# A two-layer hybrid attention trunk on one core: GpSimd casts the high part of every weight half by a copy, with its loops written out

## The reference, cut to what matters

```python
for l in range(DEPTH):
    mod = c_act @ w_mod[l] + b_mod[l]
    shift, scale, gate = jnp.split(mod, 3, axis=-1)
    h = x * (1.0 + scale[:, None, :]) + shift[:, None, :]
    p = h @ w_in[l]
    ...
    y = jnp.concatenate([y_nsa, y_gdn, y_sb], axis=-1) @ w_out[l]
    x = _layernorm(DEEPNORM_ALPHA * x + (1.0 + gate[:, None, :]) * y, ln_g[l], ln_b[l])
```

## Time and profile before

| | |
|---|---|
| time, median of 3 | 2987.98 us (2983.08 to 2988.05) |
| the profiled execution, its own time | 2985.01 us |
| its span, first to last instruction | 2983.2 us |
| mean granted TensorE clock | 0.949 |
| PE busy | 2580.8 us, 87% |
| DVE busy | 1493.6 us, 50% |
| ACT busy | 646.7 us, 22% |
| POOL busy | 1491.2 us, 50% |

### The profile page before, as it was taken

The page is one execution under the profiler, slowest core; times in us unless marked ns, Lnnn a source line. Parts: engine busy times, 40 slices in busy tenths (PEclk is TensorE's granted clock), DMA queues, the critical chain, the costliest instruction groups (busy, mean ns, idle before and its releaser), DMA issues.

```text
span 2983.2 us, 40726 instructions
## 1 busy us (share of the span) xinstructions
PE 2580.8 (87%) x14320; PEld 2030.7 (68%) x14320; DVE 1493.6 (50%) x1915; ACT 646.7 (22%) x1168; POOL 1491.2 (50%) x692
## 2 busy tenths in 40 slices
PE   0498879878999999898987999999899999997994
PEld 0376667656777777675875777777677777774773
DVE  8614751575555553565334144144655554457445
ACT  0201210112222223333003022012222222335000
POOL 7155335433444444554762644554444444553774
PEclk9999989998999999998998999999999999998997
DMA  9533343343211112444223311321111112334531
GB/s 357 211 113 107 127 143 127 113 149 99 64 56 56 56 57 76 148 137 170 93 73 115 119 57 58 120 66 55 50 57 57 57 57 63 122 121 161 188 95 71
DMA packets 82892, 314.73 MB, mean 106 GB/s; under 512 B 9974, under 2 KB 10230, under 8 KB 76950
## 3 DMA queue, kind: packets, MB, share of 16 engines
q1 hardware_dynamic: 76608, 295.51, 30.0%
q10 hardware_dynamic: 6108, 16.83, 1.6%
HBM read 303.92 MB, written 8.39 MB: 105 GB/s over the span
## 4 chain that ended last, share of the span: by engine, by line
PE 52%; DVE 20%; POOLq 12%; issue 9%; ACT 3%; DMA 2%; DVEq 1%; ACTq 1%; SPq 0%
DVE arena L1241 12%; PE bank L450 11%; PE bank L452 10%; PE bank L451 10%; POOLq L1198 7%; POOLq L1196 5%; DVE acc L1241 5%; PE bank L831 2%; PE bank L833 2%; PE bank L832 2%; PE bank L430 2%; ACT arena L843 2%; DMA ring<-in_stream 2%; DVE tiny L1241 2%; PE bank L534 1%
## 5 line engine op out<-in xcount | busy, mean ns | idle before, releaser
L1195 POOL TENSOR_TENSOR w_hi<-ring,cst 128x1024 fp32r<-128x1024 f32 (+1 forms) x328 | 622.3, 1897 | 1403.9 <-PE bank L452 892.7
L450 PE MATMUL bank<-h_hi,w_hi 128*128 128x512 f32 x2048 | 894.3, 437 | 47.5 <-POOLq L1198 44.1
L1197 POOL TENSOR_TENSOR w_lo<-ring,w_hi 128x1024 fp32r<-128x1024 f32 (+1 forms) x328 | 802.8, 2448 | 48.0 <-issue 0.4
L452 PE MATMUL bank<-h_hi,w_lo 128*128 128x512 f32 x2048 | 822.4, 402 | 0.9 <-issue 0.9
L451 PE MATMUL bank<-h_lo,w_hi 128*128 128x512 f32 x2048 | 822.5, 402 | 0.0
L450 PEld LDWEIGHTS bank<-h_hi,w_hi 128*128 128x128 f32 x2048 | 400.7, 196 | 156.6 <-POOLq L1198 46.9
L452 PEld LDWEIGHTS bank<-h_hi,w_lo 128*128 128x128 f32 x2048 | 397.8, 194 | 91.5
L451 PEld LDWEIGHTS bank<-h_lo,w_hi 128*128 128x128 f32 x2048 | 400.5, 196 | 82.3 <-issue 13.5
L843 ACT ACTIVATE arena<-bank 128x512 f32<-128x512 f32 (+6 forms) x352 | 165.8, 471 | 1031.9 <-PE bank L452 402.6
L1241 DVE SCALAR_TENSOR_TENSOR acc<-ring,cact,acc 128x1024 f32<-128x1024 f32 x128 | 213.6, 1669 | 45.8 <-DMA ring<-in_stream 29.9
L831 PE MATMUL bank<-w_hi,h_hi 128*128 128x512 f32 x512 | 202.7, 396 | 7.5 <-POOLq L1198 7.5
(11 more groups left out here) (192 smaller groups left out, 2816.9 us busy)
## 6 DMA issues: line engine op xcount, KB each, us to landing
ring<-in_stream SPq DMA_DIRECT2D x480, 512.0 KB, 3.5
yT<-in_mod SPq DMA_DIRECT2D x32, 1024.0 KB, 5.2
arena<-in_x SPq DMA_DIRECT2D x1, 4096.0 KB, 14.2
arena<-in_x ACTq DMA_DIRECT2D x4, 1024.0 KB, 10.0
x_norm<-arena ACTq DMA_DIRECT2D x4, 1024.0 KB, 9.0
arena<-x_norm ACTq DMA_DIRECT2D x4, 1024.0 KB, 9.3
out<-arena SPq DMA_DIRECT2D x4, 1024.0 KB, 3.9
raw<-in_lns ACTq DMA_DIRECT2D x8, 256.0 KB, 5.9
```

The costliest lines, as they stand in the source:

```text
L450: mm(PJ[b][:, :], hi, h_hi[:, k, :], start=(k == 0), stop=False)
L452: last = mm(PJ[b][:, :], lo, h_hi[:, k, :], start=False, stop=(k == KT - 1))
L1195: pool.tensor_tensor(w_hi[:, par, 0:w], ring[:, slot, 0:w], one.broadcast_to((P, w)), ALU.mult)
L1197: pool.tensor_tensor(w_lo[:, par, 0:w], ring[:, slot, 0:w], w_hi[:, par, 0:w].bitcast(F32), ALU.subtract)
```

## The change

The product with ones becomes a copy whose output type is float32r, and four loops of POOL become Python loops, so that all numbers in its waits are constants:

```diff
-            one = ones[:, 0:1]
...
-                pool.tensor_tensor(w_hi[:, par, 0:w], ring[:, slot, 0:w], one.broadcast_to((P, w)), ALU.mult)
+                pool.tensor_copy(w_hi[:, par, 0:w], ring[:, slot, 0:w])
...
-                with pool.Fori(0, KVH) as g:
+                for g in range(KVH):
...
-                with pool.Fori(0, GDN_H) as h:
+                for h in range(GDN_H):
...
-                with pool.Fori(0, SB_H - 2) as h:
+                for h in range(SB_H - 2):
...
-                with pool.Fori(0, TT) as n:
+                for n in range(TT):
```

## The result

The changed kernel takes 2896.27 us (median of 4 runs, 2894.21 to 2901.1), the kernel before 2985.53 us in the same comparison: the ratio is 0.9706, 95% interval 0.9686 to 0.9727, a gain of 2.9% or about 88 us. The prediction was 2947 us with a range of 2924 to 2976: right in direction, and too small by more than half. The profiled execution took 2894.2 us, its span is 2892.4 us, its mean granted clock 0.959 (0.949 before).

A forecast was written before the change was run, and what follows sets the result against it. The kernel was taken as PE-bound with holes (PE busy 87% of the span). Direct waits 13.9, DVE held by POOL 21 and clock 3 sum to 38 us, so 2985.0 - 38 = 2947 us, range 2924 to 2976.

The forecast's parts named there:

- two kinds of holes: PE's waits POOL can touch: 51.6 us for a split itself, and many for DVE (56.0 us at line 621).
- Part D: POOL's written-out loops: branches and register instructions hidden behind POOL's waits, given nothing; late code fetch bound 0 to 3 us.
- the ladder: Delta-rule heads: DVE and POOL instructions hold each other in turn; a shorter product moves the whole chain 0.74 us earlier.
- Part A: PE's 20 direct waits for POOL at lines 450 and 831: shorter splits save 13.9 us.
- Part B: PE's waits for DVE held by POOL, at lines 430, 621, 608 and 778: 21 us saved.
- Part C: PE's lower granted clock behind long waits: mostly stays, 3 us saved, bounds 0 and 8.
- The price of the copy: POOL's copy on 1024 columns: 1.15 us from the int32 CAST row, a saving of 0.74 us per split.
- my lower end: Copy priced as the 512-column MEMSET doubled: 1.04 us, a saving of 0.85 per split.
- shorter ones among the 43 waits: PE's shorter waits for DVE at line 621: about 8 us, counted only in the low end.
- my low end: Forecast's fastest time, 2924 us: a saving of 61 us with cheaper copy, full Part B and 8 of clock.
- rivals 2 and 3: Copy no cheaper, 2985 to 2988 us, chance 0.07; copy in a slow loop, slower at 3067 us, chance 0.07.
- Rival 1: Only direct waits gain, as Part B's hits cancel: 2971 us, chance 0.08.

The follow-up runs named there:

- two pieces: The change, with each half split in two pieces (copy and difference of 512 columns each), PE told after each: 2832.07 us, ratio 0.9512.
- the copy made again: The change, with 605 of the 1024 columns copied a second time before the difference: 2935.46 us, ratio 0.9856.
- the difference with an early signal: The change, copy whole, difference in two instructions of 512 columns, PE told after each: 2854.65 us, ratio 0.9591.
- the copy with a MEMSET behind it: The change, with a MEMSET of 740 columns of the low part between copy and difference: 2918.31 us, ratio 0.9802.
- The product in halves: The kernel before, its loops and product with ones kept, the product made in two instructions of 512 columns: 2968.29 us against 2979.12, ratio 0.9964.
- four-piece run: The change, with each half split in four pieces of 256 columns, PE told after each: 2896.59 us, ratio 0.9715.

## Why the prediction was wrong, point by point

Right were the way the gain takes (PE's holes, not POOL's load), the two kinds of holes, the worthlessness of the loops (Part D), and the order of the ladder. (Part D put the registers and branches at a few tenths of a us per half if nothing covered them. Where POOL went straight on to the next half it stood idle 0.33 to 0.34 us before and 0.31 after, so they cost hundredths.) The forecast fell short in the sizes of all three parts:

| term | predicted | measured |
|---|---|---|
| saving per split | 0.74 us | 0.86 (1935 to 1078 ns mean) |
| Part A, waits for POOL | 13.9 | 25.6 (51.6 to 26.0) |
| Part B, line 430 | 12 | 20.1 |
| Part B, lines 621 and 608 | 6 | 11.9 (65.6 to 53.7) |
| Part B, line 778 | 3.0 | 3.0 |
| Part B, other waits for DVE | 0 | 5.1 |
| Part C, the clock | 3 | 23.6 |

- **The price of the copy.** I had taken the CAST from int32 as the nearest row. Unheld, the float32 copy takes 1.04 us, as long as the MEMSET doubled, my lower end. That alone makes 38 into 44.
- **Part A.** The shift was about right for the first waits of layer 0 (4.03 to 3.10, 3.88 to 3.26), but three things were missing. In stick-breaking, the difference itself had been held by DVE (3.14 us where 2.34 is its own time); an earlier split misses that hold, and the long waits there fell by up to 2 us each. The four waits of 1.2 to 2.0 us vanished entirely, so that eight of my twelve are left. And three waits in the output projection fell from 2.25 to 0.64 us: the copy was issued 3.0 us behind the start of DVE's additions where the product had been issued 2.2 behind it, so it also met less of the first addition (it took 1.45 us, 0.4 over its own time, where the product took 3.16, 1.3 over).
- **Part B.** The discounts were wrong. The full shift, 20 x 0.74 = 14.8, was discounted to 12 because ACT and PE feed these chains. Measured, nine long waits lost 0.88 to 0.95 us, the ten short ones 0.82 to 0.84, and one of 2.90 us went whole. Nothing of the shift was lost. And the "shorter ones among the 43 waits", put at the low end only, belonged in the sum.
- **Part C is the step that failed worst:** 3 us, with a bound of 8, where PE's busy time fell by 23.6. I argued that the long waits of Part A stay long, so the loss behind them stays, and I looked at the waits for POOL alone. In the timeline of PE after the first 125 us, 53 waits of 2 us or more stand before the change and 29 after it. Ten of those that went are the 2.8 us waits at line 430. Behind seven of these the granted clock is now 1.00, each some 1.4 us of busy time; behind three it is as low as before or little better. That makes the 9.6 us of the delta-rule heads. Even behind waits of Part A the loss didn't all stay: in layer 1 the clock behind two of the 2.25 us waits of the output projection was 0.57, and behind the 0.64 us that are left of them it is 1.00, 1.6 us each. The rest of the 23.6 was not laid out wait by wait. The count of long waits is only a rough sign: two pieces have 16 and 2525.2 us of busy time, the copy made again 42 and 2567.6, but the difference with an early signal has 30, one more than the change, and 2530.6, 27 less.

By its own table my low end, 2924, had summed 61 us; of the missing 27, some 16 are the clock and 10 Part A.

The rivals: the copy is cheaper, so rivals 2 and 3 are out by the 1.08 us row. Rival 1, hits that cancel, is out by the waits for DVE, 40 us lower, though a few new hits did come (the 9.6 us more at line 608).

What made the product cost 88 us can be laid out in steps by the runs. From the change (0.9706) to the copy with a MEMSET behind it (0.9802): 29 us, for being 0.85 us later less what the gap for DVE gave back. From there to the copy made again (0.9856): 16 us for reading SBUF in that time; the intervals of these two runs overlap. From there to the kernel before (1): 43 us, with the waits for POOL the same. In this last step the same 1.9 us are one instruction instead of two, and it has two inputs. The product in halves shows that the cut alone, with both inputs kept, brings the waits at line 430 down by 16 us and the delta-rule heads from 848.8 to 819.2 us; the copy made again brings them to 812.5. So in these heads most of the gain is the cut's. How the rest of the 43 divides between the cut and the second input was not told apart.

## What to carry to other kernels

When two engines lock each other out for whole instructions, cost a helper's instruction by its length and by who stands behind it, not by its engine's load: ask which instruction of the other engine gets in at each gap. A shorter wait on the critical engine can pay twice, once as idle time and once in the clock behind it, so look at the granted clock behind all long waits, and not only behind those of one releaser. What a given wait costs is not fixed by its length alone: behind waits of 1.88 us the clock was 1.00 in most heads and 0.57 in another. Before making an off-path step cheaper, try cutting it in pieces with a signal for each: here two pieces gave 58 us more by the ratios, and four gave all of that back.

## What the runs showed of the hardware that was not expected

- A POOL product with a broadcast column of ones takes 1.89 us on 1024 columns, a true two-input difference 2.34, a copy with rounding to float32r 1.04.
- The copy of 256 columns takes 0.40 us where nothing holds it, of 1024 columns 1.04: 0.83 ns per column. This row is from the four-piece run:

```profile
2700.18 0.40 POOL L1196 CAST w_hi<-ring 128x256 fp32r<-128x256 f32 x1 [0.17 <-issue]
```

- The Trainium skill (GPSIMD Engine Reference, section Elementwise — side-by-side cycle accounting) puts a small loop body at 1.03 cycles per element, 0.86 ns at its 1.2 GHz; these two rows agree within 4%.
- Holding works both ways and, in these rows, by order of issue. In the output projection after the change, two DVE additions and two POOL instructions take turns. The copy takes 1.45 us instead of 1.04, and the difference, behind the second addition, 4.24 instead of 2.34:

```profile
2820.08 6.61 DVE L1240 TENSOR_TENSOR arena<-arena,raw 128x2048 f32<-128x2048 f32 x2
```

```profile
2823.09 1.45 POOL L1194 CAST w_hi<-ring 128x1024 fp32r<-128x1024 f32 x1 [1.60 <-PE bank L833]
2824.69 4.24 POOL L1196 TENSOR_TENSOR w_lo<-ring,w_hi 128x1024 fp32r<-128x1024 f32 x1
```
